# One 3 MB transfer for each routed expert behind the second shared group, issued after the down matmuls that free its slot

## The chip, the cores and the metric

The kernel runs on one core of one Trainium2 chip. The metric is the device time of one launch, in microseconds, as the median of the runs shown. A profile is one execution taken by the hardware profiler; its span runs from the first to the last instruction of the core. TensorE is PE in the rows (PEld is its weight load), VectorE is DVE, ScalarE is ACT, GpSimd is POOL, SyncE is SP, and SPq is SP's work of issuing transfers.

## The reference

A decoder trunk of two layers over 256 tokens of width 1024, all in float32. Layer 0 mixes with a gated linear recurrence, layer 1 with causal attention of 8 heads. After each mixer comes the part that the change touches, a mixture of experts:

```python
scores = sigmoid(xt @ router_w)                    # 256 tokens, 64 experts, each token takes 8
for e in experts:                                  # on the tokens that chose e
    hdn = silu(xs @ w_gate[e]) * (xs @ w_up[e])    # 1024 -> 256
    acc[tok] += (hdn @ w_down[e]) * weight         # 256 -> 1024
ffn = acc + (silu(xt @ s_gate) * (xt @ s_up)) @ s_down
```

A layer norm and a gated per-layer embedding follow. In float32 the weights of one expert are 2 MB for gate and up and 1 MB for down, 64 times 3 MB a layer.

## The kernel before

Each layer has its own mixer and then `moe(L)`, in which TensorE runs groups of experts (`expert_group`, L689) and SP loads their weights (`expert_loop`, L378). VectorE and ScalarE evict, apply silu, build one-hot matrices that gather and scatter tokens, and follow TensorE through semaphores.

**Groups and positions.** Experts are processed in an order that is computed on the chip from how many tokens chose each; a place in this order is a position, `p` or `q` in the code, 0 to 63. `SIZES` (L63) has 26 groups of 2 or 4 positions; groups 10 and 14 (`SHARED_AT`) have none and compute the shared expert. Group 19 holds positions 42 to 45, group 25 positions 56 to 59. Positions 60 to 63 are the tail, two groups of two in a loop whose count comes from a table (once in the execution profiled). A group always fills the 128 rows of the array, with 64 rows for each of two experts or 32 for each of four, so a group of four takes TensorE as long as one of two and twice as much data.

**One group on TensorE.** It waits for `gu.._loaded` of its positions, then runs the gate and up matmuls (eight steps of 128 in depth; the last one signals `gu_mm`, the one halfway `gu_front`). Then come the scatter of the group before, transposes, in odd groups the gather for the next two, and, behind a wait for `down.._loaded` (L760), the down matmuls, whose two halves each signal `down_mm`. Groups follow one another in program order.

**Slots.** Weights lie in 7 slots of 3 MB in SBUF (slot 5 is the tensor `scratch`, the rest `weights`). `ring()` (L73) gives each position its slot and `FREED_BY`, the group that had the slot before. Positions 34 and 35 (group 15) are freed by group 12, 36 to 39 (groups 16 and 17) by group 13, 40 (group 18) by the shared group 14, 41 and 42 by 15, 43 and 44 by 16, 45 and 46 by 17, 47 and 48 by 18, 49 to 52 by 19, 53 and 54 by 20, 55 by 21.

**SP's order.** SP goes through positions in pairs and issues, in program order on its one queue, the two transfers of 2 MB, each behind a wait on `gu_mm` of the group that frees the slot (L407), then the two of 1 MB, each behind a wait on `down_mm` (L413). A slot's gate and up part can so be refilled while the down part is still in use. Groups in `HALVED` (3 and 25) and the tail load gate and up in halves, the first behind `gu_front`. A transfer covers 128 partitions, one row each of 16 KB or 8 KB, 8 rows on each of 16 engines. Pairs of positions share four semaphores of each kind, `p // 2 % 4`; both transfers of a pair add 16 to the same one. Behind the loop SP loads what the next stage needs.

Of the kernel before, what the change touches and what calls it, by code (L numbers as in the profile page):

```python
# [40 lines left out]
NE, NG, EPG = 64, 8, 8  # L41
# [20 lines left out]
SHARED_AT = (10, 14)  # L62
SIZES = [0 if g in SHARED_AT else 4 if g in (4, 6, 8, 13, 19, 25) else 2 for g in range(26)]  # L63
GROUPS = len(SIZES)
HALVED = (3, 25)
STARTS = [sum(SIZES[:g]) for g in range(GROUPS + 1)]
TAIL = STARTS[GROUPS]
IN_GROUP = [g for g in range(GROUPS) for _ in range(SIZES[g])]
# [19 lines left out]
def rest_counts():  # L88

    counts, table = [0] * 4, {}  # L90
    for q in range(0, NE, 2):
        if q >= TAIL or IN_GROUP[q] in HALVED:
            counts[q // 2 % 4] += 64 if q == RESIDENT else 32
            table[q // 2] = counts[q // 2 % 4]
    return table


PIECES = {(L, c, h): [(2 * c + h, 0, HALF)] for L in range(LAYERS) for c in range(TC) for h in range(2)}
PIECES[1, 1, 1] = [(3, 0, HALF // 2), (0, HALF // 2, HALF // 2)]
GATE_UP = ("gu", "gu_rest")  # L100
SHARED_SLOT = 4
SLOT_OF, FREED_BY = ring()
assert FREED_BY[RESIDENT:RESIDENT + 2] == [0, 0]
REST = rest_counts()
assert sorted(SLOT_OF[TAIL:TAIL + 2]) == [0, 4] and sorted(SLOT_OF[TAIL + 2:]) == [5, 6]
TABLE = 4 + OVER + 8
NITER_MIN = 1
# [25 lines left out]
def build(nc, xt_d, x_d, pt_d, cst_d, cstb_d, chan_d, rows_d, tab_d, win_d, gates_d, wout_d, shared_d,  # L133
          router_d, experts_d, ple_d, pgate_d, wkv_d, wq_d, wo_d, out_d):
    ctx = ExitStack()
    with ctx:
# [117 lines left out]
        def S(name):  # L254
            if name not in names:
                names[name] = sem(name)
            return names[name]
# [9 lines left out]
        def E(s):  # L267
            if s == 5:
                return flat
            u = 15 if s == 6 else 3 * s  # L270
            return W[:, u:u + 3, :].rearrange("p a n -> p (a n)")
# [62 lines left out]
        def _(sp):  # L334
# [3 lines left out]
            def gate_up(L, p, src):  # L338
                sp.dma_start(E(SLOT_OF[p])[:, 0:GU], src[:, 0:GU]).then_inc(S(f"gu{p // 2 % 4}_loaded_{L}"), 16)
# [38 lines left out]
            def expert_loop(L):  # L378

                for q in range(RESIDENT, TAIL, 2):  # L380
                    ps = range(q, q + 2)
                    if q == FIXED:
                        sp.wait_ge(S("ordered"), L + 1)
                    if q < FIXED:
                        weights = [experts_d[L, p] for p in ps]
                    else:
                        weights = [chosen(L, sp.value_load(order[0:1, L, p:p + 1], min_val=0, max_val=NE - 1)) for p in ps]  # L387
                    if q == RESIDENT:
                        sp.wait_ge(S("gu_quarter"), L + 1)
                        for p, w in zip(ps, weights):  # L390
                            gate_up_part(L, p, w, 0, 0, KC // 4)
                        sp.wait_ge(S(f"gu_front_{L}"), 1)
                        for p, w in zip(ps, weights):
                            gate_up_part(L, p, w, 1, KC // 4, KC // 2)
                        sp.wait_ge(S(f"gu_mm_{L}"), 1)
                        for p, w in zip(ps, weights):
                            gate_up_part(L, p, w, 1, KC // 2, KC)
                    elif IN_GROUP[q] in HALVED:
                        for p, w in zip(ps, weights):
                            sp.wait_ge(S(f"gu_front_{L}"), FREED_BY[p] + 1)  # L400
                            gate_up_part(L, p, w, 0, 0, KC // 2)
                        for p, w in zip(ps, weights):
                            sp.wait_ge(S(f"gu_mm_{L}"), FREED_BY[p] + 1)
                            gate_up_part(L, p, w, 1, KC // 2, KC)
                    else:
                        for p, w in zip(ps, weights):
                            sp.wait_ge(S(f"gu_mm_{L}"), FREED_BY[p] + 1)  # L407
                            gate_up(L, p, w)
                    if q == RESIDENT:
                        sp.wait_ge(S("sorted_mm"), L + 1)  # L410
                        down(L, 4, experts_d[L, 4])
                    for p, w in zip(ps, weights):
                        sp.wait_ge(S(f"down_mm_{L}"), 2 * FREED_BY[p] + 2)  # L413
                        down(L, p, w)
                sp.wait_ge(S("table"), L + 1)
                n = sp.value_load(tab[0:1, L, 0, TABLE - 1:TABLE], min_val=NITER_MIN, max_val=NITER_MAX)
                with sp.Fori(0, n) as i:
                    for b in range(2):
                        ps = [sp.value_load(tab[0:1, L, 1, bass.ds(i * 4 + 2 * b + s, 1)], min_val=0, max_val=NE - 1)
                              for s in range(2)]  # L420
                        es = [sp.value_load(order[0:1, L, bass.ds(q, 1)], min_val=0, max_val=NE - 1) for q in ps]
                        freed = sp.value_load(tab[0:1, L, 2, bass.ds(i * 2 + b, 1)], min_val=1, max_val=4 * NE)
                        sp.wait_ge(S(f"gu_front_{L}"), freed)
                        for s in range(2):
                            gate_up_part(L, TAIL + 2 * b + s, chosen(L, es[s]), 0, 0, KC // 2)
                        sp.wait_ge(S(f"gu_mm_{L}"), freed)
                        for s in range(2):
                            gate_up_part(L, TAIL + 2 * b + s, chosen(L, es[s]), 1, KC // 2, KC)
                        freed = sp.value_load(tab[0:1, L, 3, bass.ds(i * 2 + b, 1)], min_val=1, max_val=4 * NE)
                        sp.wait_ge(S(f"down_mm_{L}"), freed)  # L430
                        for s in range(2):
                            down(L, TAIL + 2 * b + s, chosen(L, es[s]))
                sp.wait_ge(S(f"down_mm_{L}"), 2 * IN_GROUP[TAIL - 1] + 2)
                load(f"ple_{L}", ple_d[L])
                load(f"ln2_{L}", rows_d[(4 * L + 2) * D:(4 * L + 4) * D].rearrange("(a l) -> a l", a=1).broadcast_to([P, 2 * D]))
                for i in range(4):
                    load(f"pg{i}_{L}", pgate_d[L, i])
                return n
# [7 lines left out]
            n = expert_loop(0)  # L446
# [32 lines left out]
            for c in range(TC):  # L479
                for h in range(2):  # L480
                    for j, (b, i, w) in enumerate(PIECES[1, c, h]):
                        sp.wait_ge(S("x_out"), 4 + 2 * c + h + 1 + j)
# [6 lines left out]
        def _(pe):  # L489
# [7 lines left out]
            for b in range(KC):  # L497
# [6 lines left out]
                w = unit(f"win{b // 2}").rearrange("p (b k c) -> p b k c", b=2, k=KC)  # L504
# [82 lines left out]
            def moe(L):  # L587
# [98 lines left out]
                    mm(PS[0:1, 7, 0:OVER], ovs[0:OVER, 0:1], ident[0:OVER, 0:OVER], True, True  # L686
                       ).then_inc(S("over_mm"), 1)

                def expert_group(g, it, b, slots, loads, first=False, own_gather=False, next_gather=False,  # L689
                                 shared=False, rests=(), rest_at=KC // 2, by_pairs=False):  # L690

                    rows = P // len(slots)
# [64 lines left out]

                    if not first:
                        turn_weights()
                    for j, n in loads:  # L760
                        pe.wait_ge(S(f"down{j}_loaded_{L}"), n)
                    if shared:
                        arrived(pe, f"sh2_{L}")
# [14 lines left out]
                for g in range(GROUPS):  # L778
                    ps = range(STARTS[g], STARTS[g + 1])
                    expert_group(g, g // 2, g % 2, [SLOT_OF[p] for p in ps] or [SHARED_SLOT],  # L780
                                 [(p // 2 % 4, 32 * (p // 8) + 32) for p in ps[::2]], g == 0,
                                 next_gather=g % 2 == 1 and g < GROUPS - 1, shared=SIZES[g] == 0,
                                 rests=[(p // 2 % 4, REST[p // 2]) for p in ps[::2] if g in HALVED],
                                 rest_at=KC // 4 if g == IN_GROUP[RESIDENT] else KC // 2, by_pairs=g == GROUPS - 1)
                    if g == 3:
                        overflow()
                pe.wait_ge(S("table"), L + 1)
                n = pe.value_load(tab[0:1, L, 0, TABLE - 1:TABLE], min_val=NITER_MIN, max_val=NITER_MAX)
                with pe.Fori(0, n) as i:
                    for b in range(2):  # L790
                        expert_group(i * 2 + (GROUPS + b), i + ITERS, b, SLOT_OF[TAIL + 2 * b:TAIL + 2 * b + 2],
                                     [((TAIL // 2 + b) % 4, i * 32 + (32 * ((TAIL // 2 + b) // 4) + 32))], own_gather=b == 0,
                                     rests=[((TAIL // 2 + b) % 4, i * 32 + REST[TAIL // 2 + b])])
                pe.wait_ge(S(f"turned_{L}"), n * 2 + GROUPS)
                pe.wait_ge(S(f"y_out_{L}"), n * 4 + (2 * GROUPS - 1))
# [9 lines left out]
            def after(L):  # L805

                def pgate(c, h):
                    for b, i, n in PIECES[L, c, h]:
                        if b != 2 * c + h:
# [143 lines left out]
        def _(act):  # L953
# [119 lines left out]
            def gate(L, c, h):  # L1073

                for j, (b, i, n) in enumerate(PIECES[L, c, h]):
                    act.wait_ge(S("pgate_mm"), 4 * L + 2 * c + h + 1 + j)
# [668 lines left out]
```

## Time and profile before

| | |
|---|---|
| median of 3 runs | 1260.38 us (1258.57 to 1262.38) |
| span of the profiled execution | 1256.4 us (its own time outside the profile is not recorded) |
| TensorE matmul / weight load | busy 1193.9 us (95%) / 604.9 us (48%) |
| VectorE, ScalarE | busy 407.5 us, 257.9 us |
| queue q1, issued by SP and ScalarE | 456.88 MB, 87.4% of the 16 transfer engines |
| read from HBM | 459.60 MB, 367 GB/s over the span |
| 2 MB expert transfers | 90 to `weights`, 18 to `scratch` |

The page gives busy time, which for matmuls is not the same as speed, since they are pipelined. The share of the transfer engines is an average over stages: it is near full in the two expert loops (about 126 to 577 us and 765 to 1215 us) and low between them. The time from issue to landing of a transfer includes what lies in the queue ahead of it. Waits are put down to the event that ended them.

### The profile page before, as it was taken

Reading aid. Unit: us, or ns where it says so; the run is one execution under the profiler, and the core shown is the slowest. Engines: PE = TensorE matmul, PEld = TensorE weight load, DVE = VectorE, ACT = ScalarE, POOL = GpSimd, SP = SyncE. Lnnn points to the kernel's source line nnn. Section 1 sums busy time; section 2 is a strip of 40 time slices with the busy share of each in tenths; the row PEclk is TensorE's granted clock in tenths of the full one; section 3 lists DMA queues with packets and bytes.
Section 4 is the critical chain, followed back from the end, with each engine's and each line's share of the span. In section 5 each row is a group of like instructions: output and inputs, shape, how many; then the busy total and the mean of one; then the engine's idle time right before and its main releaser. Section 6 shows DMA issues by size and latency. Waiting matters only on the chain.

```text
span 1256.4 us, 15344 instructions
## 1 busy us (share of the span) xinstructions
PE 1193.9 (95%) x5946; PEld 604.9 (48%) x5946; DVE 407.5 (32%) x1096; ACT 257.9 (21%) x465; POOL 0.7 (0%) x9
## 2 busy tenths in 40 slices
PE   7999998859999999999999999997699999999998
PEld 6866444324444445444544654443244444444344
DVE  4756333112232222224311245322122222233242
ACT  1512221102211112112412411221111112112121
POOL 0000000000000000000000000000000000000000
PEclk9999999879999999999999999998899999999999
DMA  9955999999999999999822268999999999999990
GB/s 365 423 225 215 394 399 420 423 425 425 427 425 425 426 426 424 419 421 421 351 101 100 103 280 343 388 418 426 428 425 425 425 424 426 423 425 424 420 380 33
DMA packets 50042, 461.64 MB, mean 367 GB/s; under 512 B 5681, under 2 KB 6194, under 8 KB 8754
## 3 DMA queue, kind: packets, MB, share of 16 engines
q1 hardware_dynamic: 48816, 456.88, 87.4%
q10 hardware_dynamic: 1154, 3.79, 0.8%
q8 instruction: 47, 0.77, 0.3%
q14 instruction: 25, 0.20, 0.0%
HBM read 459.60 MB, written 1.05 MB: 367 GB/s over the span
## 4 chain that ended last, share of the span: by engine, by line
PE 78%; DMA 14%; SPq 3%; issue 3%; DVE 2%; ACT 0%; DVEq 0%
PE ps L491 75%; DMA weights<-in_experts 14%; SPq L343 2%; PE ps L578 1%; PE ps L748 1%; PE ps L755 1%; DMA weights<-in_win 1%; SPq L346 1%; DVE x_lo L1357 0%; DVE x_res L1286 0%; PE ps L894 0%; DVE sorting L1331 0%; SPq L387 0%; DVE z L1278 0%; DVE scratch L1278 0%
## 5 line engine op out<-in xcount | busy, mean ns | idle before, releaser
L491 PE MATMUL ps<-weights,xT 128*64 128x512 f32 (+3 forms) x2080 | 530.7, 601 | 43.9 <-issue 40.0
L491 PEld LDWEIGHTS ps<-weights,xT 128*64 128x64 f32 (+2 forms) x2080 | 183.4, 139 | 325.8 <-issue 314.7
L491 PE MATMUL ps<-weights,scratch 128*64 128x512 f32 (+2 forms) x1024 | 261.6, 597 | 1.2 <-DVE scratch L1446 1.2
L491 PE MATMUL ps<-scratch,xT 128*64 128x512 f32 (+2 forms) x384 | 157.6, 564 | 2.2 <-ACT xT L955 1.4
L491 PEld LDWEIGHTS ps<-weights,scratch 128*64 128x64 f32 (+2 forms) x1024 | 82.5, 136 | 112.1 <-issue 111.5
L1456 DVE SCALAR_TENSOR_TENSOR y_lo<-ps,slot_weight,y_hi 128x512 fp32r<-128x512 f32 x112 | 84.0, 751 | 152.6 <-ACT y_hi L955 152.6
L955 ACT ACTIVATE y_hi<-ps,slot_weight 128x512 fp32r<-128x512 f32 x112 | 76.7, 687 | 251.7 <-PE ps L491 238.9
L1443 DVE TENSOR_TENSOR scratch<-scratch,ps 128x256 f32<-128x256 f32 x56 | 23.6, 421 | 314.9 <-ACT scratch L955 314.9
L955 ACT ACTIVATE scratch<-ps 128x256 f32<-128x256 f32 (+2 forms) x68 | 26.7, 393 | 429.8 <-PE ps L491 423.1
L955 ACT ACTIVATE xT<-ps 128x512 f32<-128x512 f32 x132 | 77.5, 598 | 103.6 <-PE ps L491 84.9
L491 PE MATMUL ps<-onehot,x_hi 128*128 128x256 f32 x448 | 91.1, 289 | 0.9 <-DVE onehot L1365 0.9
L491 PE MATMUL ps<-onehot,x_lo 128*128 128x256 f32 x448 | 88.9, 282 | 0.3
L491 PEld LDWEIGHTS ps<-onehot,x_hi 128*128 128x128 f32 x448 | 69.6, 189 | 25.9 <-issue 21.3
L491 PE MATMUL ps<-y_hi,onehot_T 128*128 128x512 f32 x224 | 80.6, 438 | 0.0
L491 PEld LDWEIGHTS ps<-scratch,xT 128*64 128x64 f32 (+2 forms) x384 | 49.4, 143 | 49.4 <-issue 44.9
L491 PE MATMUL ps<-scratch 128*64 128x512 f32 (+1 forms) x160 | 72.8, 598 | 0.0
L491 PE MATMUL ps<-y_lo,onehot_T 128*128 128x512 f32 x224 | 70.7, 394 | 0.0
L491 PEld LDWEIGHTS ps<-onehot,x_lo 128*128 128x128 f32 x448 | 68.8, 190 | 0.7 <-DVE x_lo L1357 0.7
L491 PE MATMUL ps<-xT,weights 128*128 128x256 f32 x256 | 57.3, 387 | 8.9 <-DMA weights<-in_win 8.9
L1446 DVE COPY scratch<-ps 128x256 f32<-128x256 f32 x56 | 23.8, 425 | 120.5 <-PE ps L748 120.5
L491 PEld LDWEIGHTS ps<-xT,weights 128*128 128x128 f32 x256 | 49.7, 195 | 15.9 <-DMA weights<-in_win 8.9
L491 PEld LDWEIGHTS ps<-y_lo,onehot_T 128*128 128x128 f32 x224 | 42.0, 188 | 10.1 <-issue 0.5
(176 smaller groups left out, 687.9 us busy)
## 6 DMA issues: line engine op xcount, KB each, us to landing
weights<-in_experts SPq DMA_DIRECT2D x90, 2048.0 KB, 18.8
weights<-in_experts SPq DMA_DIRECT2D x140, 1024.0 KB, 24.0
scratch<-in_experts SPq DMA_DIRECT2D x18, 2048.0 KB, 20.2
scratch<-in_experts SPq DMA_DIRECT2D x24, 1024.0 KB, 21.8
weights<-in_pgate SPq DMA_DIRECT2D x8, 1024.0 KB, 27.6
weights<-in_wkv SPq DMA_DIRECT2D x8, 1024.0 KB, 26.4
weights<-in_win SPq DMA_DIRECT2D x7, 1024.0 KB, 20.5
weights<-in_shared SPq DMA_DIRECT2D x6, 1024.0 KB, 10.6
```

The lines of the kernel that those rows point to most:

```text
L343: sp.dma_start(E(SLOT_OF[p])[:, ks], src[:, ks]).then_inc(S(f"{GATE_UP[part]}{p // 2 % 4}_loaded_{L}"), 16)
L346: sp.dma_start(E(SLOT_OF[p])[:, GU:EXPERT], src[:, GU:EXPERT]).then_inc(S(f"down{p // 2 % 4}_loaded_{L}"), 16)
L491: return nc.tensor.matmul(out, lhsT, rhs, start=first, stop=last, skip_group_check=shared_bank)
L578: m = nc.tensor.transpose(PS[:, b + j, k * P:k * P + P], src[:, c, (4 * j + k) * P:(4 * j + k + 1) * P], ident)
L748: m = nc.tensor.transpose(PS[:, 6, f * P:f * P + P], hh[:, f * P:f * P + P], ident)
L755: m = nc.tensor.transpose(PS[:, 7, (2 + c) * P:(3 + c) * P], ohw[:, c, :], ident)
L955: return nc.scalar.activation(out, in_, f, **kw)
L1443: v.tensor_tensor(hh, sg, PS[:, 6, DE:2 * DE], ALU.mult).then_inc(S(f"hidden_{L}"), 1)
L1446: v.tensor_copy(hT.rearrange("p f s -> p (f s)"), PS[:, 6, 0:DE]).then_inc(S(f"hidT_{L}"), 1)
L1456: v.scalar_tensor_tensor(y_lo[:, half(h)], PS[:, 4 + h, :], wslot[:, 0:1], y_hi[:, half(h)].bitcast(F32), ALU.mult, ALU.subtract).then_inc ...
```

## The change

For positions in groups 15 to 24 (`whole(q)`), SP waits once, for both halves of the down matmuls of the group that frees the slot, and issues the expert's 3 MB as one transfer with rows of 24 KB. It counts on the `gu` semaphore; TensorE waits on that before the gate and up matmuls, and on no down semaphore for these groups. `down_counts()` gives the down semaphores' targets for the positions that still have a transfer of their own. Group 25 and the tail load as before.

```diff
--- before.py
+++ after.py
@@ -95,6 +95,21 @@
     return table
 
 
+def whole(q):
+
+    return q < TAIL and SHARED_AT[1] < IN_GROUP[q] < HALVED[1]
+
+
+def down_counts():
+
+    counts, table = [0] * 4, {}
+    for q in range(0, NE, 2):
+        if not whole(q):
+            counts[q // 2 % 4] += 32
+            table[q // 2] = counts[q // 2 % 4]
+    return table
+
+
 PIECES = {(L, c, h): [(2 * c + h, 0, HALF)] for L in range(LAYERS) for c in range(TC) for h in range(2)}
 PIECES[1, 1, 1] = [(3, 0, HALF // 2), (0, HALF // 2, HALF // 2)]
 GATE_UP = ("gu", "gu_rest")
@@ -102,6 +117,7 @@
 SLOT_OF, FREED_BY = ring()
 assert FREED_BY[RESIDENT:RESIDENT + 2] == [0, 0]
 REST = rest_counts()
+DOWN = down_counts()
 assert sorted(SLOT_OF[TAIL:TAIL + 2]) == [0, 4] and sorted(SLOT_OF[TAIL + 2:]) == [5, 6]
 TABLE = 4 + OVER + 8
 NITER_MIN = 1
@@ -402,10 +418,15 @@
                         for p, w in zip(ps, weights):
                             sp.wait_ge(S(f"gu_mm_{L}"), FREED_BY[p] + 1)
                             gate_up_part(L, p, w, 1, KC // 2, KC)
-                    else:
+                    elif not whole(q):
                         for p, w in zip(ps, weights):
                             sp.wait_ge(S(f"gu_mm_{L}"), FREED_BY[p] + 1)
                             gate_up(L, p, w)
+                    else:
+                        for p, w in zip(ps, weights):
+                            sp.wait_ge(S(f"down_mm_{L}"), 2 * FREED_BY[p] + 2)
+                            sp.dma_start(E(SLOT_OF[p]), w).then_inc(S(f"gu{p // 2 % 4}_loaded_{L}"), 16)
+                        continue
                     if q == RESIDENT:
                         sp.wait_ge(S("sorted_mm"), L + 1)
                         down(L, 4, experts_d[L, 4])
@@ -686,7 +707,7 @@
                     mm(PS[0:1, 7, 0:OVER], ovs[0:OVER, 0:1], ident[0:OVER, 0:OVER], True, True
                        ).then_inc(S("over_mm"), 1)
 
-                def expert_group(g, it, b, slots, loads, first=False, own_gather=False, next_gather=False,
+                def expert_group(g, it, b, slots, loads, downs, first=False, own_gather=False, next_gather=False,
                                  shared=False, rests=(), rest_at=KC // 2, by_pairs=False):
 
                     rows = P // len(slots)
@@ -757,7 +778,7 @@
 
                     if not first:
                         turn_weights()
-                    for j, n in loads:
+                    for j, n in downs:
                         pe.wait_ge(S(f"down{j}_loaded_{L}"), n)
                     if shared:
                         arrived(pe, f"sh2_{L}")
@@ -778,7 +799,8 @@
                 for g in range(GROUPS):
                     ps = range(STARTS[g], STARTS[g + 1])
                     expert_group(g, g // 2, g % 2, [SLOT_OF[p] for p in ps] or [SHARED_SLOT],
-                                 [(p // 2 % 4, 32 * (p // 8) + 32) for p in ps[::2]], g == 0,
+                                 [(p // 2 % 4, 32 * (p // 8) + 32) for p in ps[::2]],
+                                 [(p // 2 % 4, DOWN[p // 2]) for p in ps[::2] if not whole(p)], g == 0,
                                  next_gather=g % 2 == 1 and g < GROUPS - 1, shared=SIZES[g] == 0,
                                  rests=[(p // 2 % 4, REST[p // 2]) for p in ps[::2] if g in HALVED],
                                  rest_at=KC // 4 if g == IN_GROUP[RESIDENT] else KC // 2, by_pairs=g == GROUPS - 1)
@@ -789,7 +811,8 @@
                 with pe.Fori(0, n) as i:
                     for b in range(2):
                         expert_group(i * 2 + (GROUPS + b), i + ITERS, b, SLOT_OF[TAIL + 2 * b:TAIL + 2 * b + 2],
-                                     [((TAIL // 2 + b) % 4, i * 32 + (32 * ((TAIL // 2 + b) // 4) + 32))], own_gather=b == 0,
+                                     [((TAIL // 2 + b) % 4, i * 32 + (32 * ((TAIL // 2 + b) // 4) + 32))],
+                                     [((TAIL // 2 + b) % 4, i * 32 + DOWN[TAIL // 2 + b])], own_gather=b == 0,
                                      rests=[((TAIL // 2 + b) % 4, i * 32 + REST[TAIL // 2 + b])])
                 pe.wait_ge(S(f"turned_{L}"), n * 2 + GROUPS)
                 pe.wait_ge(S(f"y_out_{L}"), n * 4 + (2 * GROUPS - 1))
```

## Rows read from the trace of the kernel before

**Rows 1.** The page's 40 slices: share of the transfer engines, in tenths
```profile
DMA  9955999999999999999822268999999999999990
```

**Rows 2.** Windows: length, busy time of each engine, granted clock, transfer share, GB/s
```profile
363.00:438.00 75.00, 75.00 (x374) 35.20 (x376) 23.08 (x65) 13.57 (x23) 0.00 (x0) 1.00 1.01 425
438.00:512.00 74.00, 74.00 (x422) 36.46 (x413) 20.20 (x54) 15.96 (x27) 0.00 (x0) 1.00 1.01 423
```

**Rows 3.** Chain that ended last, in order of time: start, length, what
```profile
509.78 26.48 DMA weights<-in_experts
...
540.63 26.11 DMA weights<-in_experts
...
1144.06 29.70 DMA weights<-in_experts
```

**Rows 4.** PE's waits in 520:580, then 1160:1210: us, times, longest
```profile
PE ps L491 <- DMA weights<-in_experts: 1.7, 2, 1.3
...
PE ps L491 <- DMA weights<-in_experts: 2.0, 2, 1.3
```

**Rows 5.** Issues into an empty queue, at 675.8 and 616.5: KB, us to landing
```profile
weights<-in_shared SPq DMA_DIRECT2D x1, 1024.0 KB, 4.9
...
weights<-in_wo SPq DMA_DIRECT2D x1, 1024.0 KB, 4.7
```

**Rows 6.** SP's issues in order of time: start, length to the last
```profile
332.19 0.85 SPq L346 DMA_DIRECT2D weights<-in_experts  x2
...
345.17 0.33 SPq L346 DMA_DIRECT2D scratch<-in_experts  x1
345.69 0.33 SPq L346 DMA_DIRECT2D weights<-in_experts  x1
...
362.06 1.27 SPq L346 DMA_DIRECT2D weights<-in_experts  x2
...
412.32 9.71 SPq L346 DMA_DIRECT2D weights<-in_experts  x2
...
1000.42 0.85 SPq L346 DMA_DIRECT2D weights<-in_experts  x2
...
1050.71 9.70 SPq L346 DMA_DIRECT2D weights<-in_experts  x2
```

**Rows 7.** Us from issue to landing of those at 332.7, 345.7, 421.7, 1060.1
```profile
weights<-in_experts SPq DMA_DIRECT2D x1, 1024.0 KB, 15.1
...
weights<-in_experts SPq DMA_DIRECT2D x1, 1024.0 KB, 16.9
...
weights<-in_experts SPq DMA_DIRECT2D x1, 1024.0 KB, 15.3
...
weights<-in_experts SPq DMA_DIRECT2D x1, 1024.0 KB, 14.9
```

**Rows 8.** Queue q1 in 340:510, then 502:612: packets, MB, share of 16 engines
```profile
q1 hardware_dynamic: 6713, 72.01, 100.5%
...
q1 hardware_dynamic: 6278, 45.98, 100.5%
```

**Rows 9.** PE in order of time where group 19 starts, both layers
```profile
434.42 1.92 PE L491 MATMUL ps<-weights,xT 128*32 128x512 f32 x16
...
1072.78 1.06 PE L491 MATMUL ps<-weights,xT 128*32 128x512 f32 x8
```

**Rows 10.** Windows at two idle stretches of PE, columns as in rows 2
```profile
855.99:858.66 2.67, 0.00 (x0) 0.00 (x0) 1.91 (x7) 0.69 (x1) 0.00 (x0) 1.00 0.95 405
...
216.65:220.37 3.72, 0.00 (x1) 0.00 (x0) 2.45 (x9) 0.69 (x1) 0.00 (x0) 1.00 0.97 413
220.37:227.20 6.83, 3.17 (x16) 0.90 (x20) 0.00 (x0) 0.00 (x0) 0.00 (x0) 0.50 1.03 424
```

**Rows 11.** Windows of PE's gate and up matmuls of groups 19 and 6
```profile
434.40:441.50 7.10, 7.07 (x64) 1.00 1.01 427
...
224.03:232.65 8.62, 8.62 (x64) 0.82 1.03 436
```

## The prediction

> **What bounds the kernel now.** I read the span first: 1256.4 us in the profiled execution, of which no other time is known. The median of the runs is 1260.38 us, so some 4.0 us lie around the span; I keep them and add changes of the span to the median. The slices show when the transfer engines are busy: in the two long stretches of nines, which are the two expert loops [rows 1]. A window over 75 us of the first loop has both resources full: TensorE is busy for 75.00 of 75.00 us and the transfers run at 425 GB/s, share 1.01 [rows 2]. So the question is which of the two has room, and where. The chain in order of time answers it: it is TensorE work through the middle of each loop and passes to transfers at the loop's end, with pieces that end at 536.3 and 566.7 us in the first layer and at 1173.8 in the second [rows 3]. What TensorE really waits for there is small: 1.7 us in two waits in the first layer, 2.0 us in two in the second [rows 4]. Both resources therefore stand within about 2 us of the end, and this is the key: **a TensorE delay in the middle of a loop is forgiven only up to 1.7 or 2.0 us, and a gain in transfers can give back no more than these 3.7 us together, 0.29%.** About 0.3% (3.8 us) is what a measurement of this kernel can tell from no change.
>
> **The change, part by part.** It touches positions 34 to 55 (groups 15 to 24), 22 experts a layer, 44 in all. I call the gate and up matmuls of a group its front work.
>
> *The issue moves back.* Today an expert's 2 MB wait for the end of the front work of the group that frees the slot, and its 1 MB for the end of that group's down matmuls. Now everything waits for the latter. Both transfers of each expert move, past nothing but each other on SP's queue. What counts is whether the transfer engines still have work at that moment. A transfer of 1 MB issued into an empty queue lands after 4.9 or 4.7 us [rows 5]; in the stream a transfer of 1.049 MB takes 1.049/0.425 = 2.5 us [rows 2]. So issuing and completion cost 2.3 us when nothing hides them, and a transfer issued at I leaves a hole of I + 2.3 minus the landing of the one ahead of it.
> - Positions 34 and 35: the transfer ahead is the down part of position 33, second of the pair at 332.19, so issued at 332.70 [rows 6], landed 15.1 later [rows 7] at 347.8. The new issue comes with the down matmuls of group 12, where today's stands: 345.17 [rows 6]. 345.17 + 2.3 = 347.5: just in time, hole 0.
> - Positions 36 and 37: freed by group 13, whose down matmuls end just ahead of the issue at 362.06 [rows 6]. Ahead of them lies only position 35, whose down part, issued 345.69, lands after 16.9 at 362.6, now 0.2 earlier (next item) at 362.4. 362.06 + 2.3 = 364.4: **a hole of 2.0 us** that wasn't there. In the second layer the same issue stands at 1000.42 [rows 6] and the pair ahead at the same distance from it: again 2.0.
> - All later ones are issued with 2 us or more still queued: after the hole positions 36 to 39 are queued at once, four experts of 3.15 MB or 30 us. Nearest to empty is 49, freed by group 19, with some 2 us to spare. Hole 0.
>
> *Packets get longer.* Rows of 16 and 8 KB become one of 24 KB. In 340:510 q1 moves 6713 packets and 72.01 MB in 100.5% of 16 engines, in 502:612, where nearly all are 8 KB, 6278 and 45.98 MB in 100.5% [rows 8]. One packet in nine is a 4-byte increment. That leaves 5967 data packets, 2824 of them of 16 KB, in the first and 5580 in the second; the 8 KB packet comes to 0.314 us and the 16 KB one to 0.616, so two in one save 0.012. An engine takes 8 rows of an expert: 0.09 us each, 2.0 us a layer. The bounds are 0, if a row over 16 KB is cut up (no packet here is longer), and 2.4 us with the increment packets that go too. I take 2.0, the extrapolation of the two lengths seen. It happens to pay for the hole by the end of the loop, so the transfers end where they do today, give or take 0.3 us.
> The Trainium skill (DMA: Bandwidth & Descriptors, Why small descriptors are slow) gives a packet a fixed cost of about 3 fabric cycles, by the clock in Where 436 GB/s comes from some 3.5 ns; the rows show 12 ns and decide. By the page the saving would be an estimated 0.6 us a layer and the sum 1.3 us higher.
>
> *TensorE waits for more.* Today a group starts when its 2 MB parts are in and waits for the rest before its down matmuls; now it needs all 3 MB first. Most of these groups have their data early. The tight one is group 19, four experts (42 to 45). It starts at 434.42 and 1072.78 [rows 9]. The down part of position 45, today needed only some 13 us later, is the second of the pair at 412.32, issued at 421.70 [rows 6] and landed after 15.3, at 437.0 [rows 7]; in the second layer issued at 1060.1 (pair at 1050.71) and landed after 14.9, at 1075.0. After the change position 36 starts 1.8 later than today (2.0 of hole less 0.2), and ten experts of 0.09 take 0.9 back: landings 437.9 and 1075.9. With 0.1 us for the wake-up, **group 19 starts 3.5 us late in layer 0 and 3.1 in layer 1.** TensorE works without a gap from there on, 74.00 of 74.00 us up to 512 [rows 2], in group 24, so the delay is carried to where today's waits stand. Groups 20 to 24 need their last landings 1 to 3 us later than they come, once they are themselves late; nothing is added.
>
> *At the end.* Layer 0: 3.5 less the 1.7 us of waits that it uses up, 1.8. Layer 1: 3.1 - 2.0 = 1.1. After the loop everything is TensorE's chain, so both reach the end: +2.9.
>
> *The clock.* TensorE now idles 3.5 and 3.1 us in a row. In two idle stretches of today the granted clock was still 1.00 for 2.67 us in one and for 3.72 us in the other; it was 0.50 behind them, the level of 1.2 GHz [rows 10]. The new gaps of 3.5 and 3.1 lie between, so a fall in each is about an even chance or a little less. Its price: the same front work takes 7.1 us at full clock and 8.6 in a window that ran at 0.82 [rows 11], so 1.5 us, between 0 and 7.1 (all of it at the lower level). I take one fall in the two gaps: +1.5.
>
> *Costs of nothing.* SP issues 44 transfers fewer at 0.33 us each, hidden: SP mostly waits, and where its issues are held back near 500 us the transfer engines are full anyway. The dropped waits on the down semaphores cost TensorE nothing. SP's later wait delays nothing else; what stands behind it on the queue is the next pair, which waits for a later group.
>
> **Sum:** 1.8 + 1.1 + 1.5 = +4.4 on the median: 1264.8 us.
>
> **The rivals.**
> 1. *Group 19 is late but the clock holds in both gaps.* +2.9, 1263.3, no measurable change. For it: gaps barely longer than the shortest delay before a fall. Chance 0.30.
> 2. *The clock falls in both.* +5.9, 1266.3. Chance 0.12.
> 3. *No gain from long packets.* The holes stay, group 19 is later by 0.9 in each layer, and its gaps of 4.4 and 4.0 us make one fall nearly sure: 2.9 + 1.8 + 1.5 to 3.0, 1266.6 to 1268.1. For it: nothing here shows such a packet. Chance 0.11.
> 4. *The other side: no hole, and the wait at group 19 is forgiven.* Were a queued issue quicker than the 2.3 us of an idle one, position 45 would land 1.1 us earlier than today, at 435.9 and 1073.9; group 19 would be late by 1.5 and 1.2, less than the 1.7 and 2.0 at the loop's end. It decides where the delay of group 19 passes those two numbers. The transfers then end 2.0 earlier and some 0.6 us of waits go: 1259.8. Against it: the queue ahead is really down to one pair at 362. Chance 0.10.
> 5. *Every transfer has a price of its own, and 22 of them go a layer.* The gap between 4.9 alone and 2.5 in the stream, 2.4 us, would free up to 53 us of transfer time a layer, but TensorE could cash only the 3.7 us of [rows 4]: 1256.7. Against it: the stream already moves 425 GB/s with 1 and 2 MB transfers, so that price is overlapped. Chance 0.02. The Trainium skill (DMA: Bandwidth & Descriptors, Anatomy of one DMA) states such a fixed cost, about 2.0 us, for the path that GpSimd issues; by it these fewer transfers would be a gain, and the 425 GB/s speak against adding it up in a full queue.
> 6. *The change has no effect on the order of events* (TensorE further behind than in this execution). 1260.4, chance 0.02.
> The forecast has the rest, 0.33.
>
> **The numbers.** The forecast's own terms are uncertain by 1 us (hole 1.5 to 2.3, clock 1.1 to 1.7), the runs by another. From 1260.6 up to 1268.3 takes in the forecast, rivals 1 and 2 and nearly all of 3, and leaves out 4, 5, 6 and the worst of the clock's bound. Faster by over 0.3%: out of reach but by rival 5 and noise, 0.04. Within 0.3% (up to 1264.2): rivals 1, 4, 6 and a third of the forecast, 0.44. Slower: 0.52.
>
> **What would show it.** Right: a dip in the transfers' share near 362 to 364 and 1000 to 1002; a TensorE wait on a transfer at group 19 (near 434.5 and 1073) of 3 to 4 us, by far the longest new one; the waits at the end of the loops gone; packets of 24 KB taking 0.92 us; the clock at 0.50 for some us behind one of the gaps. Wrong: no wait at group 19, or one at another group; a longer hole than 2.5 us; packets cut at 16 KB; or a loop that ends later although group 19 starts on time, which would mean that the transfers got slower.

## The result and the profile after

| | before | after |
|---|---|---|
| median of 7 runs | 1259.52 us (1258.57 to 1263.41) | 1263.74 us (1262.08 to 1266.01) |
| span of the profiled execution | 1256.4 us | 1261.4 us |
| mean granted TensorE clock | 0.984 | 0.979 |
| q1: packets, share of 16 engines | 48816, 87.4% | 42480, 86.9% |

The ratio is 1.0028, 95% interval 1.0018 to 1.0038: slower, by 4.2 us between the medians, at the edge of what can be told from no change, with an interval that leaves no change out. The forecast was +4.4 us, in a range from +0.2 to +7.9. The sum is right, and as shown below it is so partly by luck, by terms that were too small on both sides. In all later runs the span is 1.8 to 1.9 us shorter than the run's own time. So the profiled execution of the kernel before probably took about 1258.3 us, less than its median, and the prediction's 4.0 us around the span were not there; the two spans differ by 5.0 us where the medians differ by 4.2. One run of whole17_not19 below took 1393.15 us at a granted clock of 0.844; its ratio is formed without it.

Four places of the new trace answer to the prediction. First TensorE where group 19 starts, in order of time, in both layers [rows 9]; the bracket is the idle time ahead and what ended it:

```profile
439.99 9.40 PE L512 MATMUL ps<-weights,xT 128*32 128x512 f32 x64 [5.35 <-DMA weights<-in_experts]
...
1080.23 1.08 PE L512 MATMUL ps<-weights,xT 128*32 128x512 f32 x4 [4.59 <-DMA weights<-in_experts]
```

It waits 5.35 and 4.59 us for position 45's whole transfer. These are the only waits of TensorE on a transfer in 420:580 and 1060:1215; the ones at the loops' ends [rows 4] are gone. The landings of three transfers ahead, from issue times and us to landing, for those issued at 332.86 (down part of position 33), at 345.85 (35) and 362.74 (37):

```profile
weights<-in_experts SPq DMA_DIRECT2D x1, 1024.0 KB, 16.0
...
weights<-in_experts SPq DMA_DIRECT2D x1, 3072.0 KB, 19.7
...
weights<-in_experts SPq DMA_DIRECT2D x1, 3072.0 KB, 18.7
```

So they land at 348.9, 365.6 and 381.4. Position 45, issued at 421.85 and 1062.85, lands 18.0 and 17.2 us later, at 439.9 and 1080.1.

Second the holes, and third the clock, in windows (length, busy time by engine, granted clock, transfer share, GB/s). The first two stand at the end of group 13's down matmuls in each layer, the third behind position 48 in layer 0; then come two stretches at the lower level of the clock:

```profile
361.80:364.00 2.20, 2.20 (x9) 1.06 (x6) 1.29 (x5) 0.69 (x1) 0.00 (x0) 1.00 0.64 164
1002.80:1004.60 1.80, 1.80 (x8) 0.87 (x5) 0.90 (x3) 0.69 (x1) 0.00 (x0) 1.00 0.87 241
...
458.90:461.00 2.10, 2.10 (x14) 0.69 (x12) 1.19 (x4) 0.69 (x1) 0.00 (x0) 1.00 0.72 203
...
437.90:444.72 6.82, 4.74 (x24) 1.35 (x28) 0.00 (x0) 0.00 (x0) 0.00 (x0) 0.50 0.98 417
1079.60:1083.00 3.40, 2.77 (x16) 0.91 (x20) 0.00 (x0) 0.00 (x0) 0.00 (x0) 0.50 1.01 434
```

425 GB/s [rows 2] fall to 164 and 241 where a hole was forecast. The third hole was not forecast: position 49 waits for group 19, and the wait and the clock had made that group's end 7.7 us late. In both gaps the clock fell to 0.50 before TensorE had its data, and its front work takes 9.40 us in layer 0 and 8.43 in layer 1 in place of 7.07 [rows 11].

Fourth the end of the loop. TensorE in order of time at group 25, before and after:

```profile
523.90 7.06 PE L491 MATMUL ps<-weights,xT 128*32 128x512 f32 x32
531.34 3.63 PE L491 MATMUL ps<-weights,xT 128*32 128x512 f32 x16 [0.38 <-DMA weights<-in_experts]
536.31 3.63 PE L491 MATMUL ps<-weights,xT 128*32 128x512 f32 x16 [1.34 <-DMA weights<-in_experts]
```
```profile
531.79 12.25 PE L512 MATMUL ps<-weights,xT 128*32 128x512 f32 x64
```

Before, the two pairs of group 25 take 7.06, 3.63 and 3.63 us with waits of 0.38 and 1.34 between, 16.0 in all. After, they take 12.25: not only are the 1.7 us of waiting gone, the same 64 matmuls take 2.1 us less when nothing stops them between the pairs. Windows show where, before and after:

```profile
532.60:534.00 1.40, 1.40 (x10) 0.41 (x8) 0.00 (x0) 0.00 (x0) 0.00 (x0) 1.00 1.01 421
```
```profile
536.95:538.35 1.40, 1.40 (x18) 0.52 (x16) 0.00 (x0) 0.00 (x0) 0.00 (x0) 1.00 1.03 421
```

Before, two matmuls start every 0.43 us all the way through. After, 16 start in the middle 1.4 us, where eight did before. As I read the start times, the first eight matmuls of the second pair run there beside the last eight of the first pair, which they can't when their weights come later.

Packets behave as forecast. In 366:437 of the new trace q1 moves, at 100.0% of 16 engines,

```profile
q1 hardware_dynamic: 1390, 30.47, 100.0%
```

which is 1236 data packets of 24 KB and one increment for eight of them: 71 us x 16 / 1236, less the increments, is 0.92 us, 0.012 less than a 16 KB and an 8 KB packet as reckoned from [rows 8].

**Where the 5.0 us of span come from.** Against the end of group 18's down matmuls (434.5 before and 434.6 after; 1072.9 and 1075.6), group 20 starts 7.7 us later in layer 0 and 6.0 in layer 1. The first matmuls behind the loop (at 586.2 and 1224.2 before, 590.0 and 1229.2 after) start later by 3.7 and 2.2: the loops' ends forgive 4.1 and 3.8. Layer 1 begins 3.8 us late but reaches group 18 only 2.8 late.

3.7 + 0.1 - 1.0 + 2.2 = 5.0. These are two executions and not two medians. From the first matmul of layer 0's loop to group 18 the ten traces of this case take 292.9 to 296.1 us, and the difference is there at group 9 already, behind the long waits for transfers at groups 6 and 8 and ahead of every edit. So a term of 1 us, such as the -1.0, need not come from the change. And of all ten traces that of the kernel before has the shortest way from group 18 to behind the loop, in both layers, so what is forgiven comes out too small against it, perhaps by 1 us a layer.

### The profile page after: what moved, and what is told of

Read it like the earlier page. It is cut to its first block, busy times and chain, and to the rows that moved or that the text cites. A ratio compares the mean times of both kernels' runs of the same rounds, so it can differ in the third digit from the quotient of the medians.

```text
span 1261.4 us, 15202 instructions
## 1 busy us (share of the span) xinstructions
PE 1195.1 (95%) x5946; PEld 606.6 (48%) x5946; DVE 407.5 (32%) x1096; ACT 258.1 (20%) x465; POOL 0.7 (0%) x9
## 3 DMA queue, kind: packets, MB, share of 16 engines
q1 hardware_dynamic: 42480, 456.88, 86.9%
## 4 chain that ended last, share of the span: by engine, by line
PE 91%; DMA 3%; issue 3%; DVE 2%; SPq 0%; ACT 0%; DVEq 0%
PE ps L512 87%; DMA weights<-in_experts 3%; PE ps L769 1%; PE ps L599 1%; PE ps L776 1%; DMA weights<-in_win 1%; DVE x_lo L1380 0%; DVE x_res L1309 0%; PE ps L917 0%; DVE sorting L1354 0%; DVE z L1301 0%; DVE scratch L1301 0%; DVE scratch L1371 0%; DVE top L1370 0%; DVE scratch L1367 0%
## 5 line engine op out<-in xcount | busy, mean ns | idle before, releaser
L512 PEld LDWEIGHTS ps<-xT,weights 128*128 128x128 f32 x256 | 50.5, 198 | 16.3 <-DMA weights<-in_win 8.9
```

The lines of the kernel that those rows point to most:

```text
L512: return nc.tensor.matmul(out, lhsT, rhs, start=first, stop=last, skip_group_check=shared_bank)
```

## The experiments

Each comparison is against the kernel before on the same chip. The ratio can differ from that of the two medians by 0.05%. The median of the kernel before was 1259.24 us beside late_two, whole17, warm19 and delay19, and 1259.93 us beside the other four. Theory A: TensorE is late at group 19 and the loop's end forgives a part. Theory B: the transfers, with holes, end later. An expectation in us belongs to a median of the kernel before of about 1259.5.

**late_two.** As late as in the changed kernel, but as two transfers, with TensorE's waits as before:

```diff
+                    elif SHARED_AT[1] < IN_GROUP[q] < HALVED[1]:
+                        for p, w in zip(ps, weights):
+                            sp.wait_ge(S(f"down_mm_{L}"), 2 * FREED_BY[p] + 2)
+                            gate_up(L, p, w)
+                            down(L, p, w)
+                        continue
```

> Group 19's late start is the loss (theory A): each expert of groups 15 to 24 is issued as late as in the changed kernel, but as 2 MB and then 1 MB, so group 19 waits only for the 2 MB of position 45, 2.5 us less, plus some 0.9 us because packets are short again. Its wait is 3.5 to 4 us in layer 0 and about 3 in layer 1, the end of the loops forgives nearly all of it: 1260 to 1261.5 us. The transfers' end sets the time (theory B): the holes stay and 2.0 us of packet time a layer come on top, some 4 us over the changed kernel, 1267 to 1268 us.

Measured 1262.82 us, ratio 1.0023 (1.0013 to 1.0034), between the two. TensorE's waits on transfers in 420:580 and in 1070:1220 (us, times, longest):

```profile
PE ps L497 <- DMA weights<-in_experts: 4.1, 2, 2.7
...
PE ps L497 <- DMA weights<-in_experts: 4.1, 2, 2.8
```

Of each 4.1 us some 2.7 stand at group 19, and the clock holds there; 1.3 stand at group 25 and are back from the kernel before. So here theory B is right in kind: the holes are there, no long packets pay for them, and group 25's last wait for a transfer ends 3.2 and 4.2 us later in the loop than in the kernel before (at 540.27 and 1181.60, counted from each loop's first matmul; 536.31 and 1173.80 before). The size is less sure: the profiled execution was the slowest of the twelve, 2.6 us over their median. Late issue alone costs nearly what the change costs. That merging the transfers wins the packets back and loses it at group 19 is how I read the two traces.

**late_two17.** The same from group 17 on, so positions 34 to 37 stay early:

```diff
-                    elif SHARED_AT[1] < IN_GROUP[q] < HALVED[1]:
+                    elif 17 <= IN_GROUP[q] < HALVED[1]:
```

> As late_two (2 MB and 1 MB issued one behind the other when the down matmuls are done), but from group 17 on, so that positions 34 to 37 are issued early and the queue doesn't run dry at 362 us. If the holes made late_two slow (transfers end the loop): no hole, the kernel before's time, 1259 to 1260. If late issue itself costs elsewhere: 1262 or more.

Measured 1260.34 us, ratio 1.0001 (0.9992 to 1.0010): no loss. The loss of late_two is that of positions 34 to 37. Their holes are in the one trace and not in the other, in windows at the end of group 13's down matmuls, late_two first:

```profile
363.17:365.30 2.13, 2.13 (x9) 0.94 (x6) 1.22 (x4) 0.69 (x1) 0.00 (x0) 1.00 0.43 100
```
```profile
361.00:365.00 4.00, 4.00 (x13) 1.82 (x10) 1.83 (x8) 0.69 (x1) 0.00 (x0) 1.00 0.99 416
```

**whole17.** The changed kernel from group 17 on:

```diff
-    return q < TAIL and SHARED_AT[1] < IN_GROUP[q] < HALVED[1]
+    return q < TAIL and 17 <= IN_GROUP[q] < HALVED[1]
```

> Only groups 17 to 24 get whole transfers, so positions 36 and 37 are issued early again and nothing is missing from the queue at 362 us. Theory A: no hole, position 45 lands about 0.7 us earlier than in the kernel before, group 19 waits 2 us in layer 0 and 1.4 in layer 1, which is forgiven, and the transfers end 1.5 us earlier in each loop: 1258.5 to 1259.7 us, the kernel before or just under. A rival, in which the wait for whole experts costs at every group and not through the hole: 1262 us or more.

Measured 1259.93 us, ratio 1.0000 (0.9990 to 1.0009): no loss. But the waits at group 19 are longer than theory A had said, 3.1 and 4.1 us against 2 and 1.4, and the clock falls at both: the front work takes 8.77 and 9.86 us. Group 20 is 4.9 and 7.0 us late in this trace, counted from group 18, and the matmuls behind the loop 1.0 and 3.2: some 3.8 us of each are forgiven, which neither 1.7 nor 2.0 us could be. By this reckoning 4.2 us are not forgiven, and the medians show no loss. How much of that is the short way of the trace before and how much an earlier end of the transfers is not shown.

**delay19.** How much the end forgives, by itself: the kernel before, TensorE delayed by 4.3 us a layer with matmuls whose result is not used:

```diff
+                    if isinstance(g, int) and g == 19:
+                        for _ in range(5):
+                            mm(bank(6), ident, cst[:, 0:HALF], True, True)
                     at_once = 2 if by_pairs else len(slots)
```

> The kernel before with the same five unused matmuls ahead of group 19, a delay of TensorE by 4.3 us a layer and nothing else. If the loop's end forgives 1.7 and 2.0 us, as the prediction had it: 2.6 + 2.3 = 4.9 us over the kernel before. If it forgives nearly 4 us in each layer, because the two halves of group 25 overlap on TensorE when both are there: 0.5 + 0.5, so 1 us over the kernel before.

Measured 1258.82 us, ratio 0.9999 (0.9990 to 1.0007). 8.6 us of added TensorE work cost nothing that can be measured, where the prediction's forgiveness would make it 4.9. The prediction's 1.7 and 2.0 us are refuted. The trace gives less than the medians: group 20 is 4.5 us late in both layers, and the matmuls behind the loop 0.9 and 1.6, so 3.6 and 2.9 were forgiven, with 0.3 and 0.6 us of waiting left at the loops' ends. Here too the short way of the trace before may be a part of it.

**delay_same.** The same with the delays of the changed kernel, 7.8 and 6.1 us:

```diff
-                        for _ in range(5):
+                        for _ in range((9, 7)[L]):
```

> The kernel before with nine unused matmuls ahead of group 19 in layer 0 and seven in layer 1: 7.8 and 6.1 us, the delays that the changed kernel's trace shows for group 19 with its wait and its slow clock together (7.7 and 6.0). If TensorE's delay alone is the loss, forgiven up to some 4 us a layer: about 3.7 + 2 = 5 us over the kernel before, as the changed kernel within 1 us, 1263.5 to 1265. If the holes in the transfers are needed for the loss: 1259 to 1260.5.

Measured 1263.37 us, ratio 1.0029 (1.0020 to 1.0038), the changed kernel's 1.0028. No transfer's code is touched, and the clock is at 1.00 over the delay and the groups behind it in both layers (windows):

```profile
433.00:461.00 28.00, 28.00 (x174) 12.90 (x172) 6.27 (x17) 4.84 (x8) 0.00 (x0) 1.00 1.01 424
1075.00:1103.00 28.00, 28.00 (x178) 12.73 (x176) 6.97 (x20) 4.84 (x8) 0.00 (x0) 1.00 1.01 424
```

In this trace group 20 is 7.9 and 6.2 us late and the matmuls behind the loop 3.8 and 2.4, so 4.1 and 3.8 are forgiven, the same as in the changed kernel. TensorE's delay is enough for the whole loss; the holes matter as the cause of part of that delay.

**warm19.** The changed kernel with the same five matmuls ahead of group 19's wait, so that they fill the gap: the edit of delay19 in the other kernel.

> The changed kernel with five matmuls whose result is not used (4.3 us) ahead of group 19's wait for its weights, in a bank that is free then. TensorE works through the gap, so the clock should stay at 1.00. Theory A with the clock in it: the gate and up matmuls of group 19 take 7.1 us instead of 9.4 and some 8.5, and 3.7 us come off the changed kernel: 1260 us. If the clock's fall is off the path, forgiven later: the changed kernel's 1263.7 us within 0.5.

Measured 1259.14 us, ratio 0.9999 (0.9988 to 1.0009). The clock over the gap and over group 19's front work (windows of TensorE alone):

```profile
428.00:442.00 14.00, 13.87 (x70) 1.00 1.02 437
438.60:445.90 7.30, 7.19 (x65) 1.00 1.01 430
```

The front work takes 7.07 us again and group 20 is 4.7 us late, in both layers. The hole is still there (179 GB/s in 361.00:363.20, 223 in 1001.00:1003.20), as are the late landing and the whole transfers, and the loss is gone: the fall of the clock is what carries the delay over what the end forgives. The third hole is gone with it: 428 GB/s in 457.00:461.00. In layer 0 the weights had come by 438.7 here, against 440.0 in the changed kernel's profile, so a part of that layer's difference (0.7 us of 7.7 - 4.7) is the landing and not the clock.

**whole20.** Whole transfers for groups 20 to 24 only (`20 <= IN_GROUP[q]` in `whole`).

> Whole transfers for groups 20 to 24 only, positions 46 to 55. No hole, group 19 starts on time, and the transfers end the loops 0.9 us earlier than in the kernel before, where TensorE waits 1.7 and 2.0 us: 1258.2 to 1259 us, 0.5 to 1.5 below the kernel before in the trace's waits at group 25. If longer packets save nothing, or TensorE is late by itself: 1259.3 to 1260.

Measured 1257.76 us, ratio 0.9986 (0.9978 to 0.9995): faster than both, and a little under the range that was expected, though the gain is only 1.8 us by the ratio. Group 19 does start on time, but TensorE waits for whole experts behind it, which was not expected: 4.5 us in four waits in layer 1, never over 2.3 us at once:

```profile
PE ps L512 <- DMA weights<-in_experts: 2.5, 2, 2.3
...
PE ps L512 <- DMA weights<-in_experts: 4.5, 4, 1.6
```

**whole17_not19.** Whole transfers for groups 17, 18 and 20 to 24 (`17 <= IN_GROUP[q] < HALVED[1] and IN_GROUP[q] != 19`).

> Whole transfers for groups 17, 18 and 20 to 24; group 19 keeps its early 2 MB and its 1 MB. No hole, no long wait at group 19, clock at 1.00, transfers 1.3 us earlier at the end of each loop: 1257.5 to 1258.7 us if the transfers set the end there, 1259.3 if TensorE does.

Measured 1258.59 us, ratio 0.9986 (0.9977 to 0.9995), the same gain. The time is as expected, its course is not: TensorE waits 4.2 us in three waits in layer 0 and 2.0 us in one in layer 1, at group 20, and behind the latter the clock is at 0.50 from 1093.4 for 3.4 us. Where the gain of these two kernels comes from is not shown. The transfers' earlier end at group 25 was the expectation; no run tested it alone, and both profiled spans (1257.6 and 1257.1 us) are longer than that of the kernel before.

## Why the prediction was right, and where it was not

- *The hole at 362 us*: right in place and cause, both layers. In size it was short. In layer 0, from position 33's landing to position 35's went 16.7 us and to position 37's another 15.8, where a pair should take 14.6: 3.3 us lost against 2.0. So the hole of "just in time" at 345 was not 0.
- *Longer packets*: right, 0.92 us and 0.012 saved.
- *Group 19 starts late*: right place, mis-sized: 5.35 and 4.59 us against 3.5 and 3.1 (3.6 and 3.2 by its own landings). In layer 0 the holes explain 1.3 us of the rest. Position 33 itself landed 1.1 us later than reckoned, 16.0 us after its issue in place of 15.1; in layer 1 this was 16.9 in place of 15.1, and the two pairs behind it took only 0.9 more than they should. This part need not be the change's: delay19, whose code there is that of the kernel before, shows 16.1 and 16.3.
- *The clock*: it fell in both gaps, which was rival 2, at 2.3 and 1.4 us of front work. The forecast had one fall at 1.5. It was costed as an addition; it is the term that decides, as warm19 shows: without it the loss is gone.
- *What the loop's end forgives*: **the step that failed.** The prediction set it at the waits of [rows 4], 1.7 and 2.0 us. It is 4.1 and 3.8 in the traces of the changed kernel and of delay_same, and enough for 4.3 a layer in delay19's median. The waits were counted, but not that the work between them takes longer when it is cut up by them: 2.1 us at group 25 in layer 0, 1.6 in layer 1.
- *Hole 0 at position 49*: wrong, since its 2 us of room were eaten by a group 19 that ended 7.7 us late.
- *After the loop all reaches the end*: right from layer 0 into layer 1. Within layer 1 the trace gives 1.0 us back ahead of group 18, where the waits of groups 6 and 8 stand; delay19's trace has the same 1.0 us without any delay to give back, so it may be no more than what two executions differ by.

The terms by the trace are 7.7 and 6.0 us of delay, against 3.5 and 3.1 with 1.5 for one fall, and 4.1, 3.8 and 1.0 given back against 1.7 and 2.0. The two errors cancel: with the measured delays and its own forgiveness the prediction would have said +10.0. That the total came out is luck; place, cause and order of events are not. Rival 2's own sum was 1266.3. Rival 4 did not happen. A ratio of 1.0028 lies within the 0.3% to which the prediction gave a chance of 0.44. That delay_same and the change agree in time and in what is forgiven, and that warm19 brings the loss back, settles cause and chain; the size of a hole from the state of the queue stays open to about 1 us.

## What to carry to other kernels

What a schedule forgives is not the sum of the waits in its trace: delay one engine on purpose, by a known amount, and read it off. When the issue of a transfer is moved later, look for the one place where the queue has nothing behind it, and for the consumer with the least time between landing and use; whole20 leaves those two places out and loses nothing, it even gains 0.14%. A wait of 4 us costs more than 4 us if the clock falls in it, and work without a use in the gap can be worth its place. Terms of 1 us from one pair of traces are no more than what two executions differ by; here only the medians and a kernel with the same delay put in could tell.

## What was not expected of the hardware

- The first packets behind an empty queue are slow. In 361.80:364.00 the engines count as 64% busy and move 164 GB/s, 39% of the full rate. That is 22.5 us of engine time for the bytes of 14.7 packets of 24 KB, so an estimated 1.5 us for each that starts there, in place of 0.92. A gap between transfers costs more than its idle time.
- The 64 gate and up matmuls of a group of four in two pairs took 14.3 us of work in layer 0 with waits between and 12.25 without, at the same clock of 1.00, because the two pairs then run beside each other for a while.
- Idle stretches of 5.35 and 4.59 us came with a fall of the clock to 0.50 for 6.8 and 3.4 us. Gaps of 2.7 us in late_two did not. Shorter ones did, 2.3 us in whole20 and 2.0 in whole17_not19, and in whole20 the clock was at 0.50 only from 454.6 on, when TensorE had been at work again for 1.1 us. So the length of a gap alone doesn't tell, and the prediction's reading of 2.67 us as the shortest was too sure.

```profile
451.20:453.40 2.20, 0.00 (x0) 0.00 (x0) 1.42 (x5) 0.69 (x1) 0.00 (x0) 1.00 1.04 439
454.60:458.00 3.40, 3.40 (x10) 0.98 (x8) 0.00 (x0) 0.00 (x0) 0.00 (x0) 0.50 1.03 439
```
